# Packing 32 experts into 24 blocks of 96 + 32 rows in a mixture-of-experts stage

## The reference

```
lg = t @ w_rg + b_rg; gsel = argmax(lg)                 # one of 4 groups
le = (t @ w_re + b_re)[group gsel]; top_v, top_i = top_k(le, 2)
gate = softmax(top_v) * softmax(lg)[gsel]               # 2 of 32 experts a token
act = silu(t @ w_gate[e]) * (t @ w_up[e]) * gate        # w_gate, w_up: 1024 x 256
y  += act @ w_down[e]                                   # w_down: 256 x 1024
```

## Time and profile before

| | us |
|---|---|
| median of 3 runs (1497.73 to 1502.58) | 1500.32 |
| the profiled execution | 1503.73 |
| its span | 1501.9 |
| TensorE busy | 1323.7 (88%) |
| VectorE busy | 796.8 (53%) |
| ScalarE busy | 289.4 (19%) |
| GpSimd busy | 186.3 (12%) |
| DMA | 228 MB, 152 GB/s over the span |

### The profile page before, as it was taken

How to read it: one execution, slowest core, us unless ns; L and a number is a source line. 1 busy time by engine, 2 the same in 40 slices (tenths; PEclk the granted TensorE clock), 3 DMA queues, 4 the chain that set the end, 5 groups by cost and what they waited for, 6 DMA issues and landing times.

```text
span 1501.9 us, 14666 instructions
## 1 busy us (share of the span) xinstructions
PE 1323.7 (88%) x4897; PEld 712.9 (47%) x4897; DVE 796.8 (53%) x2237; ACT 289.4 (19%) x827; POOL 186.3 (12%) x228
## 2 busy tenths in 40 slices
PE   7978799999999947797999999988799999999980
PEld 3434445555555423353556565555345445444440
DVE  1105788999899993222344444444253244443536
ACT  1113234433433331120111110110011111111110
POOL 0000001010100001000000000000100231432405
PEclk9988799999999968798999999997799999999995
DMA  8692000300000121453016110022198999999956
GB/s 320 243 359 77 1 22 1 140 29 29 1 29 15 31 108 45 165 205 121 21 40 210 42 43 14 15 98 92 42 328 301 352 354 362 345 367 349 369 173 218
DMA packets 131076, 228.12 MB, mean 152 GB/s; under 512 B 17096, under 2 KB 95862, under 8 KB 130979
## 3 DMA queue, kind: packets, MB, share of 16 engines
q1 hardware_dynamic: 115819, 207.24, 39.5%
q0 software_dynamic: 14608, 17.87, 3.7%
q10 hardware_dynamic: 576, 2.10, 0.4%
HBM read 218.36 MB, written 45.25 MB: 176 GB/s over the span
## 4 chain that ended last, share of the span: by engine, by line
PE 76%; DVE 13%; issue 4%; DMA 3%; ACT 2%; POOL 1%; SPq 1%; DVEq 0%; ACTq 0%; POOLq 0%
PE bank L712 23%; PE bank L1121 15%; PE bank L1082 8%; PE bank L1127 8%; DVE W L1524 6%; PE bank L911 3%; PE bank L1060 2%; PE bank L1116 2%; PE bank L1020 2%; PE bank L755 2%; DVE G L1959 2%; DVE G L1469 1%; PE bank L824 1%; PE bank L1096 1%; DMA W<-in_cache_mem_k 1%
## 5 line engine op out<-in xcount | busy, mean ns | idle before, releaser
L712 PE MATMUL bank<-W,G 128*128 128x512 f32 (+3 forms) x864 | 356.7, 569 | 4.2 <-DVE G L1469 3.4
L1524 DVE SCALAR_TENSOR_TENSOR W<-W,dwT 128x128 f32<-128x128 f32 (+1 forms) x1080 | 280.4, 337 | 0.0
L712 PEld LDWEIGHTS bank<-W,G 128*128 128x128 f32 (+1 forms) x864 | 159.2, 187 | 178.2 <-issue 172.1
L1121 PE MATMUL bank<-W 128*128 128x512 f32 x528 | 235.7, 600 | 7.8 <-issue 6.1
L1121 PEld LDWEIGHTS bank<-W 128*128 128x128 f32 x528 | 100.0, 192 | 139.4 <-issue 136.9
L911 PE MATMUL bank<-W 128*128 128x512 f32 (+1 forms) x288 | 129.9, 610 | 11.7 <-DVE W L1630 7.8
L594 POOL TENSOR_SCALAR st<-st 128x1 f32<-128x1 f32 (+5 forms) x58 | 13.3, 229 | 953.6 <-DVE st L1600 278.1
L1082 PE MATMUL bank<-W 128*128 128x512 f32 (+1 forms) x288 | 128.3, 599 | 0.8 <-DVE W L1790 0.6
L1127 PE MATMUL bank<-W 128*128 128x512 f32 x264 | 122.2, 607 | 0.9 <-ACT W L1421 0.9
L1945 DVE TENSOR_TENSOR W<-bank,cvec 128x512 f32<-128x512 f32 x66 | 42.6, 686 | 138.9 <-PE bank L1116 138.8
L1959 DVE SCALAR_TENSOR_TENSOR G<-W,dwT,G 128x1024 f32<-128x1024 f32 (+1 forms) x72 | 92.2, 1281 | 14.9 <-issue 9.3
(11 more groups left out here) (271 smaller groups left out, 1364.0 us busy)
## 6 DMA issues: line engine op xcount, KB each, us to landing
W<-in_w_exp_gate SPq DMA_DIRECT2D x33, 1024.0 KB, 11.6
W<-in_w_exp_up SPq DMA_DIRECT2D x33, 1024.0 KB, 15.1
W<-in_w_exp_down SPq DMA_DIRECT2D x33, 1024.0 KB, 14.0
y_scratch<-W SPq DMA_DIRECT2D x33, 512.0 KB
y_scratch<-LG SPq DMA_DIRECT2D x1, 8192.0 KB
W<-in_cache_mem_k SPq DMA_DIRECT2D x8, 1024.0 KB, 5.2
W<-in_cache_mem_v SPq DMA_DIRECT2D x8, 1024.0 KB, 7.5
W<-in_w_in SPq DMA_DIRECT2D x4, 1792.0 KB, 24.9
```

Source lines behind the costliest of these rows:

```text
L712: mm = pe.matmul(bank[0:rows, at:at + hi - lo], HT[:, c, 0:rows], w[:, c, lo:hi], start=(c == 0), stop=(c == DC - 1))
L1121: mm = pe.matmul(B[2 + par][:, :], HG[par][:, c, :], WGU[u][:, c, :], start=(c == 0), stop=(c == DC - 1))
L1524: dve.scalar_tensor_tensor(y, src, w, y, ALU.mult, ALU.add).then_inc(M["conv_tap"], 1)
```

## The change

A block has 128 rows as before, and now of two experts. Experts come in groups of four; the fourth is cut in three parts. Block 3q + r holds up to 96 rows of expert 4q + r (r = 0, 1, 2) in its rows 0 to 95, and part r of expert 4q + 3, up to 32 rows, in its rows 96 to 127. That is 24 blocks. What an expert has beyond 96 rows goes to overflow blocks of 128 rows. Four of them are run always (`STATIC_OVER`), up to 18 more in the conditional loops.

In `gate_up` and `down` each matmul of a shared block is three, with the stationary columns 0 to 63, 64 to 95 and 96 to 127; the last takes its moving operand from the other expert's slot. They write the same PSUM bank, on the partitions of the same numbers. Overflow blocks have one full tile.

The weights are read such that each partition's part is contiguous in DRAM: row p * 8 + c of gate goes to partition p, chunk c (before: row c * 128 + p). Therefore the rows' features are permuted the same way: z3 is written transposed within the row (`by_row`), as is the activation ahead of down, and the router's weights and norm_ffn_g are read in that order. Gate and up have separate halves of a slot.

`weight_plan` works out ahead which weights go to which slot and after which block a slot is free. Gate and up of the next weights are loaded once the block's gate/up matmuls are done, down after its y is stored. There are 36 loads of an expert (32 + 4), and three combine passes over 8, 8 and 12 (and more) blocks.

```diff
-NB = NE + 1
-PASSES, PER_PASS = 4, 8
+WIDE, PART = 96, 32
+NR = NE * 3 // 4
+STATIC_OVER, OVER = 4, 22
+NB = NR + STATIC_OVER
+EVEN, ODD = (NB + 1) // 2, NB // 2
+PASSES, PER_PASS = 3, 8
...
+def weight_plan():
+    need = []
+    for q in range(NE // 4):
+        need += [("e", 4 * q + 3)] + [("e", 4 * q + r) for r in range(3)]
+    need += [("o", k) for k in range(STATIC_OVER)]
...
+    for u in range(4):
+        place(need[u], u)
+    rest = need[4:]
+    for n in range(NB):
+        freed[n] = []
+        for w in uses[n]:
+            if last[w] == n and rest:
+                freed[n].append(rest[0])
+                place(rest.pop(0), slot[w])
+    return need, uses, slot, landed, freed, count
...
-        WGU = [view(W, a, DC, 2 * FE) for a in SLOT]
+        WGU = [view(W, a, 2, DC, FE) for a in SLOT]
...
+        def expert_rows(name, e, c):
+            rows = i[name][0, e] if isinstance(e, int) else i[name][0, bass.ds(e, 1)].rearrange("o a b -> (o a) b")
+            return rows.rearrange("(p c) n -> p c n", c=c)
+        def load_gate_up(eng, e, u):
+            eng.dma_start(WGU[u][:, 0], expert_rows("w_exp_gate", e, DC)).then_inc(wgu_in[u], 16)
+            eng.dma_start(WGU[u][:, 1], expert_rows("w_exp_up", e, DC)).then_inc(wgu_in[u], 16)
+        def load_down(eng, e, u):
+            eng.dma_start(WD[u], expert_rows("w_exp_down", e, 2)).then_inc(wdn_in[u], 16)
+        def by_row(rows, c):
+            return rows.rearrange("p (c f) -> p f c", c=c)
...
             for n in range(NB):
...
+                if n + 1 < NB and FREED[n + 1]:
+                    sp.wait_ge(M["gu_done"], n + 2)
+                    for w in FREED[n + 1]:
+                        load_gate_up(sp, expert_id(w), WSLOT[w])
                 store_y(n)
-                if n + 4 < NE:
-                    load_expert(sp, n + 4, n % 4, wexp_in[n % 4])
...
+                for w in FREED[n]:
+                    load_down(sp, expert_id(w), WSLOT[w])
...
-            with sp.Fori(1, OVER) as n:
+            with sp.Fori(1, OVER - STATIC_OVER + 1) as n:
...
+            def tiles_of(n):
+                if n >= NR:
+                    return [(0, 128, WSLOT[USES[n][0]])]
+                u, part = (WSLOT[w] for w in USES[n])
+                return [(0, 64, u), (64, WIDE, u), (WIDE, 128, part)]
-            def gate_up(u, par):
+            def gate_up(tiles, par):
                 for c in range(DC):
-                    mm = pe.matmul(B[2 + par][:, :], HG[par][:, c, :], WGU[u][:, c, :], start=(c == 0), stop=(c == DC - 1))
+                    for lo, hi, u in tiles:
+                        mm = pe.matmul(B[2 + par][lo:hi, :], HG[par][:, c, lo:hi], WGU[u][:, :, c, :], start=(c == 0), stop=(c == DC - 1), skip_group_check=True)
...
-                        mm = pe.matmul(B[6 + half][:, :], AT[par][:, c, :], WD[u][:, c, 512 * half:512 * half + 512], start=(c == 0), stop=(c == 1))
+                        for lo, hi, u in tiles:
+                            mm = pe.matmul(B[6 + half][lo:hi, :], AT[par][:, c, lo:hi], WD[u][:, c, 512 * half:512 * half + 512], start=(c == 0), stop=(c == 1), skip_group_check=True)
...
                 if s4 == NT - 1:
-                    dve.tensor_copy(idx_i[:, 0:NE], IDXA).then_inc(M["route_ready"], 1)
+                    slots = idx_i[:, 0:NR].rearrange("p (q r) -> p q r", r=3)
+                    table = IDXA.rearrange("p (q r) -> p q r", r=4)
+                    for r in range(3):
+                        dve.tensor_copy(slots[WIDE:128, :, r], table[PART * r:PART * r + PART, :, 3])
+                    dve.tensor_copy(slots[0:WIDE], table[0:WIDE, :, 0:3]).then_inc(M["route_ready"], 1)
...
-                    dve.tensor_scalar(Z3[0:n3, :], XR[s3 % 4][0:n3, :], st[0:n3, 41:42], None, ALU.mult).then_inc(M["z3_ready"], 1)
+                    dve.tensor_scalar(by_row(Z3[0:n3, :], DC), XR[s3 % 4][0:n3, :].rearrange("p (f c) -> p f c", c=DC), st[0:n3, 41:42], None, ALU.mult).then_inc(M["z3_ready"], 1)
...
-                return dve.tensor_tensor(a, B[2 + p][:, FE:2 * FE], e, ALU.mult)
+                return dve.tensor_tensor(by_row(a, 2), B[2 + p][:, FE:2 * FE].rearrange("p (f c) -> p f c", c=2), e.rearrange("p (f c) -> p f c", c=2), ALU.mult)
```

More of the change, by code:

```diff
@@ L80, in rows_of, with place @@
     return NS if s == 0 else 128
+def weight_plan():
[3 more added lines that the diff above has]
+    need += [("o", k) for k in range(STATIC_OVER)]
+    uses = {}
+    for n in range(NR):
+        uses[n] = [("e", 4 * (n // 3) + n % 3), ("e", 4 * (n // 3) + 3)]
+    for k in range(STATIC_OVER):
+        uses[NR + k] = [("o", k)]
+    last = {w: n for n, ws in uses.items() for w in ws}
+    slot, count, landed, freed = {}, [0] * 4, {}, {}
+    def place(w, u):
+        slot[w] = u
+        count[u] += 1
+        landed[w] = count[u]
+    for u in range(4):
[8 more added lines that the diff above has]
+    return need, uses, slot, landed, freed, count
+NEED, USES, WSLOT, LANDED, FREED, LOADS = weight_plan()
 def build(nc, i, o):
@@ L220, in build @@
         RE2, RG8, RE3, R_EID = rt(2 * NT, NE), rt(2 * NT, 8), rt(OVER, NE), rt(OVER)
+        R_Q, R_LAST, R_PT = (rt(2 * NT) for _ in range(3))
         R_GE, R_PM = rt(PASSES + 1, 2 * NT), rt(PASSES, 2 * NT)
@@ L536, in _ @@
                     sp.wait_ge(M["mvb_used"], DEC_B)
-                    for e in range(2):
-                        load_expert(sp, e, e, wexp_in[e])
+                    for u in range(2):
+                        load_gate_up(sp, NEED[u][1], u)
+                        load_down(sp, NEED[u][1], u)
                 if s1 == NT - 1:
                     sp.wait_ge(M["mq_done"], AFTER["mq_done"] + 2 * NT)
-                    load_expert(sp, 2, 2, wexp_in[2])
+                    load_gate_up(sp, NEED[2][1], 2)
+                    load_down(sp, NEED[2][1], 2)
             sp.wait_ge(M["mo_done"], AFTER["mo_done"] + 2 * NT)
-            load_expert(sp, 3, 3, wexp_in[3])
+            load_gate_up(sp, NEED[3][1], 3)
+            load_down(sp, NEED[3][1], 3)
             def store_y(n):
@@ L550, in store_y, with expert_id @@
                 sp.dma_start(y_d[g][(n - PER_PASS * g) * 128:(n - PER_PASS * g + 1) * 128, :], YB[n % 2]).then_inc(y_out[n % 2], 16)
+            over_e = {}
+            def expert_id(w):
+                kind, k = w
+                if kind == "e":
+                    return k
+                if k not in over_e:
+                    over_e[k] = sp.value_load(eid_i[0:1, k:k + 1], min_val=0, max_val=NE - 1)
+                return over_e[k]
+            sp.wait_ge(M["gu_done"], 1)
+            for w in FREED[0]:
+                load_gate_up(sp, expert_id(w), WSLOT[w])
             for n in range(NB):
@@ L669, in _ @@
                     gather_y(q)
-            for n in range(NB - 2, NE):
+            for n in range(NB - 2, NB):
                 for q in comb_at(n):
                     gather_y(q)
-            pool.wait_ge(zg_in[0], 16 * (NE // 2 + 1))
+            pool.wait_ge(zg_in[0], 16 * EVEN)
             pool.wait_ge(M["zt4_done"], 2 * NB)
             total = pool.value_load(eid_i[0:1, OVER:OVER + 1], min_val=0, max_val=OVER)
-            with pool.Fori(1, OVER) as n:
+            with pool.Fori(1, OVER - STATIC_OVER + 1) as n:
                 with pool.If(total > n):
-                    pool.tensor_copy(idxs[:, 0:1], idx_i[:, bass.ds(n + NE, 1)]).then_inc(M["idx_copied"], 1)
+                    pool.tensor_copy(idxs[:, 0:1], idx_i[:, bass.ds(n + (NR + STATIC_OVER - 1), 1)]).then_inc(M["idx_copied"], 1)
                     pool.wait_ge(M["idx_copied"], n)
@@ L1159, in expert_step @@
                     pe.wait_ge(M["yb_readyD"], n)
-                for mm in down(n % 4, p):
+                weights_of(n, wdn_in, 16, WDN_AFTER)
+                for mm in down(tiles_of(n), p):
                     mm.then_inc(M["dn_done"], 1)
@@ L1188, in _ @@
                     pe.wait_ge(M["over_atr"], AFTER["over_atr"] + n)
-                    for mm in down(0, 0):
+                    pe.wait_ge(wdn_in[0], n * 16 + (WDN_AFTER + 16 * LOADS[0]))
+                    for mm in down([(0, 128, 0)], 0):
                         mm.then_inc(M["over_dn"], 1)
@@ L1429, in _ @@
             total = act.value_load(eid_i[0:1, OVER:OVER + 1], min_val=0, max_val=OVER)
-            with act.Fori(1, OVER) as n:
+            with act.Fori(1, OVER - STATIC_OVER + 1) as n:
                 with act.If(total > n):
```

101 lines of the change are left out of this document (55 added, 46 removed).

## The result

The changed kernel takes 1766.1 us (median, 1763.4 to 1770.2) against 1500.5: ratio 1.176, 95% interval 1.172 to 1.180. It is slower by 266 us. The forecast was 1479; the time is that of rival (a), which stood at 1770 with a chance of 0.25.

The account below looks back on a forecast made before the run. TensorE and DMA bound the expert stage almost equally, DMA most steps after the change. Stage end -23.3 us, tail +1.5, small start costs, total -21.3: 1503.7 - 21.3 - 3.4 = 1479; own range 1455 to 1496, with rival (a) 1440 to 1780.

Parts of the forecast that it names:

- rival (a): Shared blocks: TensorE drains at every change of width, 25.3 us a block, whole kernel about 1770 us; chance 0.25.
- the price of a chunk in a shared block: Gate/up and down matmuls: widths 64 and 32 overlap fully, 0.86 us a chunk (high bound 2.02), 11.7 us a shared block.
- DMA as the bound: Expert stage: transfers grow by 6% while TensorE's side shrinks by 13%, so DMA bounds most steps.
- The transfers: Expert stage: 130.6 MB at 375 GB/s take 348 us, to 1424.6; half of the new bytes in 8 KB rows.
- From there to the last copy's end: End of the expert stage: 6.9 us for the last gate/up and 12.6 after it, ending at 1441.3 against 1464.6.
- rival (c): Expert stage: DMA exceeds 400 GB/s, TensorE ends every step, 326 + 13 us, whole kernel 1443; chance 0.08.
- The tail: Before the first combine: VectorE passes 18 empty overflow turns instead of 15, 0.49 us each, +1.5 us.
- The routing operations: Block 1 on VectorE: 13 more small operations, some 3 us, cost nothing because VectorE is busy 150 of 356 us.
- The z3 write: Before the stage: transposed write, 0.744 us before, bounded by 1.29; one of nine on the last chain, +0.5 us.
- The activation's strided write: Expert stage: 0.41 us before the change, lies hidden under 6.9 us of gate/up.
- The start of the stage: First gate/up at 1066.6 instead of 1065.4, with +0.7 us for the block table's cast and +0.5 for z3.
- The zero fill: Overflow area grows from 8 to 11 MB, holding SyncE 8.8 us more; covered by 23 us of slack, otherwise up to 9.

Follow-up runs that it names:

- e1: Changed kernel with the wide tile cut in two, so shared blocks use four stationary tiles of 32 columns: 1477.1 us, ratio 0.983 to the kernel before.
- e3: Changed kernel with two tiles of 64 columns in shared blocks, rows 64 to 95 using the wrong expert's weights: 1478.0 us, ratio 0.983.
- e7: Kernel before with each gate/up and down matmul split into tiles of 64, 32 and 32 columns using the same weights: 1944.4 us, ratio 1.290.
- e8: e1 with seven eighths of each up transfer inside the stage left out (first four experts whole), 29 MB less to move: 1453.9 us, ratio 0.964.
- e2: Changed kernel with the same three tiles reordered, all chunks of the wide tile first, then all of the two narrow ones: 1707.9 us, ratio 1.135.
- e4: e1 with the contiguous weight order undone: gate and up in 1 KB pieces, z3 and activation written plainly: 1493.9 us, ratio 0.994.
- e5: Kernel before with the change's contiguous weights and matching row order alone, blocks and loads as before: 1495.8 us, ratio 0.993.
- e9: e1 with the down part of a freed slot loaded ahead of the store of the block's output: 1479.6 us, ratio 0.984.
- e11: e1 run once more, unchanged: 1476.6 us, ratio 0.983.

## Why the prediction was wrong

**The step that failed** is the price of a chunk in a shared block. I bounded it by 0.86 and 2.02 us and took 0.86. Measured: 15.88 / 8 = 1.99. The upper end, built from L930's leftover of 0.15 after each narrow run, was right to 2%.

**The argument for it** was that every change of layout seen to drain was between footprints that share columns, while L911 and L930 ran together on disjoint ones. Both facts were true, but the second pair had the same width, 64. The trace had a sample for "different instructions" and none for "different widths", and I let the first stand for the second. After e1, e3 and e7 it is settled for these fp32 matmuls: 32 beside 32 overlaps with the same weights (the two narrow tiles of e7) and with another expert's (e1), 64 beside 64 overlaps with another expert's (e3); 64 and 32 do not, on disjoint columns, with the same weights (e7).

The Trainium skill (TensorEngine Tiling (Array Packing), Tiling Modes, Key Properties) had it: a change of tiling mode drains, a change of tile does not. The traces agree: 1.99 us a chunk when the width changes, 0.86 when it doesn't. I quoted it and gave it 0.25. A page that speaks of exactly the case that no row shows should have weighed more than an analogy between rows.

**The rest of (a)** held: blocks 25.06 for 25.3, DMA share 0.55 for about 0.6, all from the first block on; total 1766 for 1770.

**DMA as the bound** was half right, as e1 shows, which is the kernel I had in fact predicted: 1477.1 for 1479. Three gaps and two waits on weights cost it the 23 us that e8 gives back, but most of its steps are still 11.68 us of TensorE without a wait. That the sum came out is luck: its terms miss in both directions. In e1's trace:

- The stage started at 1062.6, 4 us earlier than in the sum.
- The transfers were done at about 1400 (DMA share 0.97 from 1390 to 1400, 0.28 in the next 10 us) and not at 1424.6. The rate was 393 GB/s where I took 375; and down's weights too are read in 8 KB rows now, so three quarters of the bytes were in such rows and not half (e1's page has 13933 packets of 8 KB and more; 36 loads x 3 x 128 rows are 13824).
- From there to the last copy's end I had 17 us, one gate/up and what follows. It took 32, to 1431.8. TensorE's chain has no wait for weights from 1340.95 on: the last weights landed well ahead of their use, and TensorE set the end. Its stage is what rival (c) gave, 326 + 13 = 339 us, with 23.6 us of waits for weights and slow gate/ups behind them and 5.1 us for the step with `route_slots`: 368 for a measured 369.
- The tail was 3 us longer than in the sum.

The Trainium skill's figure of about 358 GB/s for a core's HBM (DMA: Bandwidth & Descriptors, Specifications) is exceeded by 393 over 324 us, reads and writes together.

**The routing operations** stood at nothing, because VectorE is busy for only 150 of 356 us. A share over a stretch says nothing about one step: in block 1 the function and the activation had 0.4 us to spare before, and its 15 more operations cost 5.1 us wherever the matmuls are fast (e1, e8).

**Small terms.** The terms of the sum add up to -21.8, not -21.3. The z3 write went to 1.337 us (bound 1.29, so +0.6 for +0.5). The tail: from the last copy's end to the first combine 13.0 us with 18 empty turns, 9.3 with 15 before; so +3.6 for +1.5. The 0.49 a turn was misread: from 1464.60 to 1472.00 the chain walks 13 of the 15 turns. The activation's strided write takes 0.60 for 0.41, hidden. The start of the stage was foreseen at 1066.6 and was 1063.3; it lies between 1062.4 and 1068.1 in the profiles of all these kernels. The zero fill cost nothing that can be seen.

## What to carry to other kernels

Count the widths of the stationary tiles, not only their columns: tiles that should run side by side must have the same width, and three unequal ones were twice as slow as four equal ones (25.06 against 11.68 us a block). When a trace shows only like beside like, the unlike pair is unmeasured; one edit of one line measures it. Small operations added to a little-used engine are free only if they fit into the one step in which they stand. And where a merged work item saves one engine's time, ask what the other bound does: 5 blocks fewer were worth 50 us of TensorE, and e1 got 23 to 28 of them; 23 more came when there was less to move (e8).

## What the runs showed of the hardware

- A visit to a layout costs 0.13 us beyond its rounds (e2 against the changed kernel: 1.88 us for 14 changes).
- The extra instructions of four tiles of 32 are free: 64 records in the 6.87 us of 16 or 32 records (e1, before, e3). A block takes 11.68 us instead of 11.40; the 0.28 are two more changes of layout, since its transposes use the full width.
- DMA moved 415 GB/s over 100 us with weights in 8 KB rows beside stores and gathers of 4 KB rows (e1), 376 with gate and up in 1 KB pieces in the same kernel (e4).
- After gaps of 5.3, 4.2 and 4.0 us in e1 a gate/up of 6.87 us took 9.93, 8.77 and 9.95. The granted clock over these was 0.71, 0.81 and 0.71, so part of each ran at the lower level.
- A conditional turn that is not taken costs VectorE a steady 0.53 us in the kernel before and 0.68 in the changed one. With the pauses between, 15 such turns and what leads to the first combine took 9.3 us in the kernel before, 10.9 in e5 and 8.6 in e7, whose loops are the same; 18 took 13.0 in the changed kernel, e1, e4, e9 and e11, and 15.5 in e8. I don't know why they differ.
